# Retention's group norm: mean taken away on ScalarE, root and gate applied in one pass on VectorE

## The reference

```python
q = rotary(q.reshape(B, T, RET_HEADS, RET_HEAD_DIM))
k = rotary(k.reshape(B, T, RET_HEADS, RET_HEAD_DIM)) * RET_HEAD_DIM ** -0.5
v = v.reshape(B, T, RET_HEADS, RET_HEAD_DIM)
o_ret = group_norm_heads(chunkwise_retention(q, k, v)).reshape(B, T, RET_WIDTH)
y_ret = o_ret * jax.nn.silu(g_ret)

def group_norm_heads(o):
    mu = jnp.mean(o, axis=-1, keepdims=True)
    var = jnp.mean(jnp.square(o - mu), axis=-1, keepdims=True)
    return (o - mu) * lax.rsqrt(var + NORM_EPS)
```

## Time and profile before

| | |
|---|---|
| median of three runs | 1716.5 us (1715.56, 1716.5, 1716.86) |
| the profiled execution | 1715.31 us |
| its span in the trace | 1713.4 us |
| PE busy | 1672.2 us (98%) |
| DVE busy | 1256.7 us (73%) |
| ACT busy | 832.5 us (49%) |
| mean granted clock of TensorE | 0.998 |
| stretch in which retention's norms lie | about 99 to 192 us |

### The profile page before, as it was taken

How to read it: one execution, slowest core, us unless ns; L and a number is a source line. 1 busy time by engine, 2 the same in 40 slices (tenths; PEclk the granted TensorE clock), 3 DMA queues, 4 the chain that set the end, 5 groups by cost and what they waited for, 6 DMA issues and landing times.

```text
span 1713.4 us, 25211 instructions
## 1 busy us (share of the span) xinstructions
PE 1672.2 (98%) x9824; PEld 1429.5 (83%) x9824; DVE 1256.7 (73%) x2201; ACT 832.5 (49%) x1346; POOL 0.2 (0%) x4
## 2 busy tenths in 40 slices
PE   7999999999999999999999999999999999999998
PEld 7888888777787778889888888889778989979997
DVE  7899767774779798856877786347756786678774
ACT  6665545553324344344444442336453455466653
POOL 0000000000000000000000000000000000000000
PEclk9999999999999999999999999999999999999999
DMA  8646542231234344542545556224222344546553
GB/s 334 232 160 223 198 145 87 79 143 62 63 96 169 115 149 165 210 144 91 145 135 196 197 196 221 93 80 136 99 86 63 122 159 144 172 156 174 196 195 125
DMA packets 79078, 254.91 MB, mean 149 GB/s; under 512 B 14320, under 2 KB 18672, under 8 KB 78320
## 3 DMA queue, kind: packets, MB, share of 16 engines
q1 hardware_dynamic: 73488, 244.91, 42.7%
q10 hardware_dynamic: 5472, 8.39, 1.5%
HBM read 252.19 MB, written 1.07 MB: 148 GB/s over the span
## 4 chain that ended last, share of the span: by engine, by line
PE 79%; DVE 13%; ACT 4%; issue 3%; DMA 1%; ACTq 0%; DVEq 0%
PE bank L693 66%; DVE w_lo L1725 3%; PE bank L824 3%; PE bank L995 2%; PE bank L981 2%; PE bank L1073 2%; PE bank L972 2%; ACT w_hi L1180 1%; PE bank L786 1%; DVE mod_w L1780 1%; PE bank L1062 1%; DVE probT L1780 1%; DMA w_raw<-in_weights 1%; DVE att L2273 1%; DVE bank L2271 0%
## 5 line engine op out<-in xcount | busy, mean ns | idle before, releaser
L1725 DVE TENSOR_TENSOR w_lo<-w_raw,w_hi 128x1024 fp32r<-128x1024 f32 (+1 forms) x356 | 427.0, 1211 | 258.7 <-ACT w_hi L1180 257.1
L1180 ACT ACTIVATE w_hi<-w_raw 128x1024 fp32r<-128x1024 f32 (+1 forms) x356 | 370.0, 1048 | 343.8 <-PE bank L693 292.0
L693 PE MATMUL bank<-hT_hi,w_hi 128*128 128x512 f32 (+1 forms) x1280 | 446.0, 348 | 1.7 <-issue 0.6
L693 PE MATMUL bank<-hT_hi,w_lo 128*128 128x512 f32 (+1 forms) x1280 | 437.6, 342 | 0.0
L693 PE MATMUL bank<-hT_lo,w_hi 128*128 128x512 f32 (+1 forms) x1280 | 437.3, 342 | 0.0
L693 PEld LDWEIGHTS bank<-hT_hi,w_hi 128*128 128x128 f32 x1280 | 242.7, 190 | 30.2 <-issue 3.1
L693 PEld LDWEIGHTS bank<-hT_hi,w_lo 128*128 128x128 f32 x1280 | 242.6, 189 | 28.2
L693 PEld LDWEIGHTS bank<-hT_lo,w_hi 128*128 128x128 f32 x1280 | 242.8, 190 | 27.0 <-issue 1.0
L1780 DVE SCALAR_TENSOR_TENSOR mod_w<-mod_w,c_rows 128x1024 f32<-128x1024 f32 x96 | 117.0, 1219 | 7.0 <-DMA mod_w<-in_mod_weights 7.0
L693 PE MATMUL bank<-w_hi,hT_hi 128*128 128x512 f32 x272 | 114.6, 421 | 0.0
L693 PE MATMUL bank<-w_lo,hT_hi 128*128 128x512 f32 x272 | 106.6, 392 | 0.0
(11 more groups left out here) (370 smaller groups left out, 2787.5 us busy)
## 6 DMA issues: line engine op xcount, KB each, us to landing
w_raw<-in_weights SPq DMA_DIRECT2D x356, 512.0 KB, 4.0
mod_w<-in_mod_weights SPq DMA_DIRECT2D x96, 512.0 KB, 3.9
nbias<-in_window_bias ACTq DMA_DIRECT2D x32, 128.0 KB, 3.0
resid_c<-in_ctx ACTq DMA_DIRECT2D x2, 1024.0 KB, 5.4
gain_mix<-gain_rows SPq DMA_DIRECT2D x3, 512.0 KB, 5.9
gain_ffn<-gain_rows SPq DMA_DIRECT2D x3, 512.0 KB, 4.0
c_rows<-in_conditions SPq DMA_DIRECT2D x1, 1024.0 KB, 5.7
gatew<-in_gate_weights SPq DMA_DIRECT2D x1, 1024.0 KB, 11.5
```

The costliest lines, as they stand in the source:

```text
L693: mm = pe.matmul(held[key][:, oc], st, mv_, start=(opens and k == 0 and t == 0 and i == 0), stop=(closes and k == tiles - 1 and t == 2), s ...
L1180: a.activation(w_hi[:, p % RING, :, used], w_raw[:, p % RING, :].rearrange("p (k n) -> p k n", k=KP)[:, :, used], ACT.Copy).then_inc(hi_re ...
L1725: v.tensor_tensor(w_lo[:, p % RING, :, used], w_raw[:, p % RING, :].rearrange("p (k n) -> p k n", k=KP)[:, :, used], w_hi[:, p % RING, :, ...
```

## The change

The norm is computed in two parts. DVE now writes the negated mean and the negated variance of both tiles into `less`, a part of `bnst` (one instruction in the place of the addition of EPS). ACT takes the root with scale -1 and EPS as bias, waits (from head 2 on) until the transposes of head h - 2 have read the slot of `onrm`, and writes `onrm` as output minus mean from PSUM in two Identity passes with a pointer bias; the second passes the bank on. DVE forms the reciprocal meanwhile. `ret_gate` waits for ACT's passes (`centred`) and multiplies `onrm` by the reciprocal root and by the gate in one scalar_tensor_tensor for each tile. The wait for the transposes of head h - 2, and the `ahead` in front of it, leave DVE.

```diff
@@ ret_sqrt on ScalarE
                 ahead(("ro", h))
                 act.wait_ge(*ret_var.at(h))
-                a.activation(bnst[:, h % 2, 6:8], bnst[:, 2 + h % 2, 0:2], ACT.Sqrt).then_inc(*A.tell(ret_root, h))
+                less = bnst[:, 2 + h % 2, 4:8].rearrange("p (t m) -> p t m", t=NT)
+                a.activation(bnst[:, h % 2, 6:8], less[:, :, 1], ACT.Sqrt, scale=-1.0, bias=eps[:]).then_inc(*A.tell(ret_root, h))
+                if h >= 2:
+                    act.wait_ge(*filled_at(("ry", h - 2)))
+                for t in range(NT):
+                    a.activation(onrm[:, h % 2, t * P:(t + 1) * P], psum(("ro", h))[:, t * P:(t + 1) * P], ACT.Identity,
+                                 bias=less[:, t, 0:1]).then_inc(*(A.drain(("ro", h)) if t == NT - 1 else A.next()))
+                A.mark(centred, h)
@@ ret_norm and ret_gate on VectorE
-                key = ret_stats(h)
-                ps = psum(key)
-                mu = att[:, 2 * (h % 2):2 * (h % 2) + 2, 0]
-                v.tensor_scalar(bnst[:, 2 + h % 2, 0:2], att[:, 2 * (h % 2):2 * (h % 2) + 2, 1], EPS, None, ALU.add)\
-                    .then_inc(*W.tell(ret_var, h))
+                ret_stats(h)
+                less = bnst[:, 2 + h % 2, 4:8].rearrange("p (t m) -> p t m", t=NT)
+                v.tensor_scalar(less, att[:, 2 * (h % 2):2 * (h % 2) + 2, 0:2], -1.0, None, ALU.mult).then_inc(*W.tell(ret_var, h))
                 dve.wait_ge(*ret_root.at(h))
                 v.reciprocal(bnst[:, 2 + h % 2, 2:4], bnst[:, h % 2, 6:8]).then_inc(*W.next())
+
+            def ret_gate(h):
+
                 dve.wait_ge(*W.last())
-                if h >= 2:
-                    ahead(("ry", h - 2))
-                    dve.wait_ge(*filled_at(("ry", h - 2)))
+                dve.wait_ge(*centred.at(h))
                 for t in range(NT):
-                    v.tensor_scalar(onrm[:, h % 2, t * P:(t + 1) * P], ps[:, t * P:(t + 1) * P], mu[:, t:t + 1],
-                                    bnst[:, 2 + h % 2, 2 + t:3 + t], ALU.subtract, ALU.mult)\
-                        .then_inc(*(W.drain(key) if t == NT - 1 else W.next()))
-
-            def ret_gate(h):
-
-                dve.wait_ge(*W.last())
-                o = onrm[:, h % 2, :].rearrange("p (t c) -> p t c", t=NT)
-                v.tensor_tensor(o, o, sg[:, :, h * P:(h + 1) * P], ALU.mult).then_inc(*W.tell(ret_y, h))
+                    o = onrm[:, h % 2, t * P:(t + 1) * P]
+                    v.scalar_tensor_tensor(o, o, bnst[:, 2 + h % 2, 2 + t:3 + t], sg[:, t, h * P:(h + 1) * P], ALU.mult, ALU.mult)\
+                        .then_inc(*(W.tell(ret_y, h) if t == NT - 1 else W.next()))
```

More of the change, by code:

```diff
@@ L448, in build @@
     lru_a = Counter("lru_a")
+    centred = Counter("centred")
     lru_clamped = Counter("lru_clamped")
@@ L496, in build @@
                fT_hi_ready, fT_ready, ffn_prod, ffn_silu, floor_ready, gate_used, h1_ready, hT_hi_ready, hT_ready,
-               hT_tmp_ready, k_ready, lam_ready, lam_scaled, log_ready, lru_a, lru_clamped, lru_e2, lru_gated, lru_hi,
+               hT_tmp_ready, k_ready, lam_ready, lam_scaled, log_ready, lru_a, centred, lru_clamped, lru_e2, lru_gated, lru_hi,
                lru_ix, lru_mult, lru_y, merged_hi, merged_ready, merged_sum, ml_e, ml_exp, ml_root, ml_ss, ml_w_ready,
@@ L1851, in ret_norm @@
             def ret_norm(h):
-                key = ret_stats(h)
-                ps = psum(key)
-                mu = att[:, 2 * (h % 2):2 * (h % 2) + 2, 0]
-                v.tensor_scalar(bnst[:, 2 + h % 2, 0:2], att[:, 2 * (h % 2):2 * (h % 2) + 2, 1], EPS, None, ALU.add)\
-                    .then_inc(*W.tell(ret_var, h))
+                ret_stats(h)
+                less = bnst[:, 2 + h % 2, 4:8].rearrange("p (t m) -> p t m", t=NT)
+                v.tensor_scalar(less, att[:, 2 * (h % 2):2 * (h % 2) + 2, 0:2], -1.0, None, ALU.mult).then_inc(*W.tell(ret_var, h))
                 dve.wait_ge(*ret_root.at(h))
                 v.reciprocal(bnst[:, 2 + h % 2, 2:4], bnst[:, h % 2, 6:8]).then_inc(*W.next())
-                dve.wait_ge(*W.last())
-                if h >= 2:
-                    ahead(("ry", h - 2))
-                    dve.wait_ge(*filled_at(("ry", h - 2)))
-                for t in range(NT):
-                    v.tensor_scalar(onrm[:, h % 2, t * P:(t + 1) * P], ps[:, t * P:(t + 1) * P], mu[:, t:t + 1],
-                                    bnst[:, 2 + h % 2, 2 + t:3 + t], ALU.subtract, ALU.mult)\
-                        .then_inc(*(W.drain(key) if t == NT - 1 else W.next()))
             def ret_gate(h):
                 dve.wait_ge(*W.last())
-                o = onrm[:, h % 2, :].rearrange("p (t c) -> p t c", t=NT)
-                v.tensor_tensor(o, o, sg[:, :, h * P:(h + 1) * P], ALU.mult).then_inc(*W.tell(ret_y, h))
+                dve.wait_ge(*centred.at(h))
+                for t in range(NT):
+                    o = onrm[:, h % 2, t * P:(t + 1) * P]
+                    v.scalar_tensor_tensor(o, o, bnst[:, 2 + h % 2, 2 + t:3 + t], sg[:, t, h * P:(h + 1) * P], ALU.mult, ALU.mult)\
+                        .then_inc(*(W.tell(ret_y, h) if t == NT - 1 else W.next()))
             def ret_lo(h):
```

## The result

The changed kernel's median is 1719.55 us (20 runs, 1717.43 to 1723.11); the kernel before, run beside it, has 1716.07 (20 runs, 1714.99 to 1720.51). The ratio is 1.0019 with a 95% interval of 1.0013 to 1.0025, so the change costs some 3 us (2.2 to 4.3 by the interval, 3.5 by the medians): more than the 1.5 of the forecast, and just inside what I had called no difference (0.2%). The profiled execution took 1719.49 us with a span of 1717.7 and a mean granted clock of 0.996.

What follows compares the result with a forecast made beforehand. PE was taken to hold 79% of the chain of waits, with VectorE and ScalarE setting most of 80 to 181 us. Sg's +1.31 and the gate's +0.18 gave +1.49, so 1718.0 us against the median 1716.5; range 1715.6 to 1719.6.

Steps and rivals of the forecast that it cites:

- the forecast: Whole kernel: 1.5 us slower through heads 4 and 5, 1718.0 us against the median; chance 0.66.
- no difference (0.2%): Whole kernel: a difference under 0.2% (3.4 us) can't be told from no change; chance of same 0.90.
- Root and pair: ScalarE, each head: root +0.09 us, two Identity passes +0.54, so what follows starts 0.63 later (0.61 to 0.83).
- Heads 0 to 3: VectorE saves 0.58 us in heads 0 and 1, but w_lo near 131 us ends up at +0.05.
- (1): Rival: VectorE rules throughout, ScalarE's additions lie in idle time, all 2.9 us of PE's waits close: 1713.6; chance 0.08.
- (2): Rival: gain and loss cancel, as (1) up to 172 us and as forecast behind it: 1716.5; chance 0.14.
- The gate of head 4: Near 181 us: sg +1.31 us, gate pair +0.18, so PE's transposes start 1.49 later and its stop is 1.8.
- it decides from somewhere between 2.2 and 3.6 us on: PE's granted clock falls only behind stops longer than a bound between 2.2 and 3.6 us; 1.8 is under both.
- Rival (3): PE's stop at 181 us grows to 1.8 us and its clock falls; price 2.5 us, 1720.5; chance 0.06.
- Clock 1.00 at all later stages: Sign the forecast is right: all stages behind head 4 later by 1.5 us, with PE's granted clock at 1.00.
- the range: Whole kernel: 1715.6 to 1719.6 us, leaving out (1), Rival (3) and (4), 0.16 together.
- (4): Rival on ScalarE: Identity and root throw each other's table out, four loads ahead of 181 us, 5 us: 1723; chance 0.02.

Runs made afterwards that it cites:

- sg_first: late_centre, with Silu of head 4's gate straight behind root 5, ahead of w_hi, and VectorE's gates ahead of w_lo; median 1716.17 us, ratio 0.9999.
- before: The kernel without the change, the reference for the comparisons; median 1716.07 us over 20 runs beside the changed kernel.
- after: The changed kernel with the new norm in all eight heads, against the kernel without it; median 1719.55 us, ratio 1.0019, profiled execution 1719.49 us.
- not45: Changed kernel with the old norm in heads 4 and 5 and the new one in the other six; median 1716.83 us, ratio 1.0003.
- only45: Changed kernel with the new norm in heads 4 and 5 only and the old one in the others; median 1718.44 us, ratio 1.0015.
- fill_before: Kernel without the change, plus two surplus float32 matmuls on TensorE in its stop at the second block's norm; median 1715.23 us, ratio 0.9994.
- after_again: The changed kernel run once more, unchanged, beside the last three experiments; median 1718.84 us, ratio 1.0020 against the kernel without the change.
- late_centre: Changed kernel with head 4's centring behind the two w_hi after its root and head 5's behind the Silu; median 1716.41 us, ratio 1.0004.

## Why the prediction was right in its mechanism and short in its size

**Root and pair.** The root is 0.09 us longer (0.30 for 0.20) as said. A pair adds 0.49 between its start and that of w_hi, where I took 0.54: one pass is 0.352 us, the mean over sixteen in the view of groups, the low end of my 0.35 to 0.47. So each head adds 0.57 or 0.58 instead of 0.63, root 5 comes at +0.58 instead of +0.68 (head 4's start was not at +0.05 but at 0), and sg at +1.18 instead of +1.31. The Trainium skill (page "ScalarE: Activation LUTs", section "What ACT_TABLE_LOAD costs") led to an estimate of 0.59 for the pair; the row has 0.49. The Trainium skill (same page, section "Rules for kernel authors") puts additions on VectorE. The change as made is slower, as that rule has it, but by the place of the passes in ScalarE's queue: in sg_first the same passes on ScalarE cost PE nothing at head 4.

**Heads 0 to 3.** The timeline of DVE at head 1, against the earlier trace rows:
```profile
108.65 0.61 DVE L1874 SCALAR_TENSOR_TENSOR onrm<-onrm,bnst,sg 128x128 f32<-128x128 f32 x2 [0.41 <-ACT onrm L1272]
109.18 0.42 DVE L1880 TENSOR_TENSOR mix_lo<-bank,mix_hi 128x256 fp32r<-128x256 f32 x1
```
What follows the gate is 0.51 us earlier (109.18 for 109.69) where I had 0.58. Head 3's stop is gone, and at 131 us the gain too:
```profile
130.60 1.23 DVE L1733 TENSOR_TENSOR w_lo<-w_raw,w_hi 128x1024 fp32r<-128x1024 f32 x1 [0.52 <-ACT w_hi L1181]
```
That is 0.02 us before the 130.62 of the earlier trace rows; I had said 0.05 after it. Root 3 came 0.62 us sooner where I had 0.58, and what it pushes 0.57 later where I had 0.63. PE runs 0.7 us ahead of before until 137 us and is back in step by 149. This was the step that set my forecast against rivals (1) and (2), and it held.

**The gate of head 4.** The pair of scalar_tensor_tensor ends 0.18 us later than the old gate, as worked out from the earlier trace rows. The failed step stands just ahead of it: I had let the gate follow sg at the old distance. It came 0.37 later, a term of the sum that was missing, and more than makes up for the shorter pairs: 1.18 + 0.37 + 0.18 = 1.73 for 1.31 + 0.18 = 1.49. The stop is 2.13 us for 1.8.

**The clock.** The sentence that failed is "it decides from somewhere between 2.2 and 3.6 us on". I had one stop of 2.17 us with a clock of 1.00 behind it and took it for a bound. It was one case of several: the same stop, 2.13 us in after, has the clock at 0.62 and 0.52 behind it:
```profile
240.15 1.10 PE L787 MATMUL bank<-diag,resid_x 128*128 128x128 f32 x5 [2.13 <-DVE diag L2047]
```
Nor does the other end hold. In not45, only45 and fill_before the stop of 3.6 us that ends near 95 us is the same as before, and the stretch behind it has a clock of 1.00 where the earlier trace rows have 0.50 (not45):
```profile
96.00:100.00 4.00, 4.00 (x36) 4.00 (x35) 3.86 (x9) 3.63 (x4) 0.00 (x0) 1.00 0.38 130
```
PE is then 2 us ahead and stops for longer at the transposes of head 3: 2.36 us in only45 and 2.37 in fill_before, with the clock at 0.50 behind it (128 to 130 us), and 2.07 in not45 with 1.00. So the length of a stop alone doesn't settle it in these traces.

Rival (3) was therefore no rival to the forecast but an addition to it, in some executions at head 4 and in some at the norm. Its price is 1.4 us and not 2.5: PE's lateness grows by 1.41 us across the fall in after, by 1.42 in only45 and by 1.42 in sg_first. The Trainium skill (page "TensorE: Matmul & The Clock Gate", section "Part 1: The HAM clock gate") says that the monitor behind the clock looks on a free-running beat, so that the same kernel meets it differently from run to run. The traces agree in so far as one kernel at one place shows both: after has the fall behind the norm's stop (2.13 us, 0.62), after_again has none (2.18 us, 1.00). "Clock 1.00 at all later stages" was wrong in the profiled execution, right in that of after_again.

**The sum.** The median of after lies 1.5 us over the forecast in the first set (1719.55) and 0.8 in the second (1718.84), the first at the edge of the range (1719.6). That it still lies inside is luck: the upper end had 1.0 us put on it for the scatter of runs, and neither the gap ahead of the gate nor a fall of the clock had been counted. Of the excess over the kernel before's median, +3.5 and +2.5, the path is 1.7 to 1.8. The rest is falls of the clock in more executions than before and the half us of small shifts; how it divides between them in the medians is not settled.

**The other rivals.** (1) and (2) fell with not45 and the 130.60 above: (2) needs a gain of some 1.5 us ahead of 172 us, and PE is back in step with before there in after and in not45. (4) didn't come: no load stands between root and Identity.

## What to carry to other kernels

Work moved to an engine that is half idle isn't free if it is put ahead of something there that a third engine waits for: ask for each instruction behind it in the queue who waits for it, and put the moved work behind the urgent ones (late_centre takes back 1.0 of 1.7 us, sg_first all of it, with the same passes). A stop that one profile shows without a fall of the clock is no bound on when the clock falls: if a stop grows to the size of ones that are already there, count the fall in with a chance, and look at the spread of the runs and not at one trace. And compare a filled kernel with a filled one: a filling that helps both would else be put down to the change.

## What the runs showed of the hardware

- An Identity pass of 128x128 from PSUM with a pointer bias takes 0.352 us alone and 0.25 us in a row. A root of 128x2 takes 0.30 us with a pointer bias and 0.20 without.
- A gate on DVE whose last operand was ready started 0.41 us after it, and 0.06 us after it when four instructions more stood 180 us earlier in DVE's stream. A change of the number of instructions on an engine can so cost or give 0.35 us on the critical path at a place that has nothing to do with it.
- The profiled executions have 16 stops of PE of 2.07 to 2.37 us (ten at the norm, three at head 4, three at head 3). Behind seven of them the granted clock fell to its lower level (1.2 GHz) for a few us, and behind nine it stayed at 2.4 GHz. Around the stop of 3.6 us that ends near 95 us it fell in 11 of 14. Where PE is the bound a fall cost 1.4 us. With two surplus matmuls in the norm's stop (1.88 us of PE) the clock stayed up behind it in all four profiled executions that had them.
- Falls of the clock between 94 and 131 us, which 13 of 14 profiled executions have, cost nothing at the end: in not45, which has none, PE runs up to 2.7 us ahead of before and is back in step by 149 us, for VectorE is the bound there.
